# One level of Strassen's scheme for the gate features of a fused attention layer

## What is computed

```python
p = rmsnorm(x, g) @ w_in                 # (1088, 2048) x (2048, 10064)
qa, ka, va, qi, wi, ki, za, qb, kb, vb, zb, ga, gb = split(p)
score = sum_h relu(qi_h . ki) * wi_h      # the indexer
keep  = top_k(score, 256)                 # keys that each query of branch A attends to
oa = attend(qa, ka, va, keep, bias);  ob = window_attend(qb, kb, vb, sinks, bias)
m  = sigmoid(ga) * ((oa * silu(za)) @ w_br_a) + sigmoid(gb) * ((ob * silu(zb)) @ w_br_b)
y  = rmsnorm(x + m @ w_out, final_g)
```

## Time and profile before

| | |
|---|---|
| median of 3 runs | 3377.52 us (3373.89 to 3378.17) |
| the profiled execution: its own time | 3377.38 us |
| its span, first to last instruction | 3375.6 us |
| PE busy | 3148.7 us (93%) |
| DVE, ACT, POOL busy | 1325.3, 850.0, 881.5 us |
| mean granted TensorE clock | 0.967 |
| ACT cast of a 128x512 quarter, mean | 620 ns |
| DMA over the span | 91 GB/s |

### The profile page before, as it was taken

One profiled execution on the slowest core, in us unless ns is written; L12 is line 12 of the kernel. 1 busy time (PEld: TensorE's weight loads), 2 busy tenths in 40 slices (PEclk: granted clock), 3 DMA queues, 4 the chain that ended last, 5 costly groups with the idle time before them and its releaser, 6 DMA issues. The chain is left out here.

```text
span 3375.6 us, 47356 instructions
## 1 busy us (share of the span) xinstructions
PE 3148.7 (93%) x17837; PEld 2975.9 (88%) x17837; DVE 1325.3 (39%) x2169; ACT 850.0 (25%) x1753; POOL 881.5 (26%) x652
## 2 busy tenths in 40 slices
PE   5999999999999999999999987975778999999997
PEld 5999999999999999999999986754667999978875
DVE  5003362737282721695000007754994111120411
ACT  4112112131312212211011115533653111031422
POOL 1222211122121222122122214422552222143453
PEclk7999999999999999999999998986998999999999
DMA  4232322222222222222633224234325333263442
GB/s 145 81 98 61 84 62 70 79 64 79 59 69 76 61 79 74 58 63 77 103 98 87 80 64 118 57 88 91 69 55 161 117 111 115 72 227 101 143 159 100
DMA packets 356871, 308.47 MB, mean 91 GB/s; under 512 B 34744, under 2 KB 316440, under 8 KB 353224
## 3 DMA queue, kind: packets, MB, share of 16 engines
q1 hardware_dynamic: 328384, 244.02, 25.9%
q10 hardware_dynamic: 28360, 62.72, 6.6%
HBM read 232.31 MB, written 74.43 MB: 91 GB/s over the span
## 5 line engine op out<-in xcount | busy, mean ns | idle before, releaser
L594 PE MATMUL banks<-h_hi,w_in_tile_hi 128*128 128x384 f32 (+3 forms) x3664 | 823.4, 331 | 10.0 <-POOL w_in_tile_lo L464 7.5
L594 PE MATMUL banks<-h_lo,w_in_tile_hi 128*128 128x384 f32 (+3 forms) x3664 | 821.2, 330 | 0.0
L594 PE MATMUL banks<-h_hi,w_in_tile_lo 128*128 128x384 f32 (+3 forms) x3664 | 821.1, 330 | 0.0
L464 POOL TENSOR_TENSOR w_in_tile_lo<-w_in_tile_raw,w_in_tile_hi 128x512 fp32r<-128x512 f32 x312 | 406.2, 1303 | 1541.5 <-ACT w_in_tile_hi L484 1541.5
L594 PEld LDWEIGHTS banks<-h_hi,w_in_tile_hi 128*128 128x128 f32 (+1 forms) x3664 | 633.4, 188 | 23.0 <-POOL w_in_tile_lo L464 8.1
L594 PEld LDWEIGHTS banks<-h_hi,w_in_tile_lo 128*128 128x128 f32 (+1 forms) x3664 | 631.4, 187 | 1.2
L594 PEld LDWEIGHTS banks<-h_lo,w_in_tile_hi 128*128 128x128 f32 (+1 forms) x3664 | 628.5, 187 | 1.6
L484 ACT CAST w_in_tile_hi<-w_in_tile_raw 128x512 fp32r<-128x512 f32 x312 | 192.9, 620 | 1347.2 <-PE banks L594 1264.1
L761 DVE MAX8 top<-score 128x8 f32<-128x384 f32 (+6 forms) x224 | 247.1, 1103 | 33.0 <-DVE score L764 1.1
L764 DVE MATCH_REPLACE8 score<-top,score 128x384 f32<-128x384 f32 (+6 forms) x224 | 242.9, 1084 | 0.0
L2102 PE MATMUL banks<-w_out_tile_hi,m_hi 128*128 128x512 f32 x576 | 226.5, 393 | 14.9 <-DVE m_lo L2032 13.2
(11 more groups left out here) (243 smaller groups left out, 3570.3 us busy)
## 6 DMA issues: line engine op xcount, KB each, us to landing
w_in_tile_raw<-in_w_in SPq DMA_DIRECT2D x312, 256.0 KB, 2.9
product<-spill ACTq DMA_DIRECT2D x70, 544.0 KB, 3.4
w_out_tile_raw<-in_w_out SPq DMA_DIRECT2D x128, 256.0 KB, 3.1
u_b<-product SPq DMA_DIRECT2D x32, 544.0 KB, 6.2
merged<-u_b ACTq DMA_DIRECT2D x16, 544.0 KB, 7.4
x_rows<-in_x_prompt SPq DMA_DIRECT2D x8, 1024.0 KB, 5.3
b_q_raw<-product SPq DMA_DIRECT2D x16, 512.0 KB, 7.5
w_br_tile_raw<-in_w_br_b SPq DMA_DIRECT2D x64, 128.0 KB, 2.9
```

What stands on the lines that cost most here:

```text
L464: pool.tensor_tensor(s.w_lo[:, q, :, :], s.w_raw[:, q, :, :], s.w_hi[:, q, :, :].bitcast(F32), ALU.subtract).then_inc(lo_made, 1)
L594: last = pe.matmul(ps[0:m, 3 * slot + c, 0:w], w_[:, q, kq, 0:m], h_[:, k, t0:t0 + w], start=(k == 0 and w_ is s.w_hi and h_ is s.h_hi), s ...
```

## The change

The 32 gate tiles leave `project`, which is left with 46 tiles. `project` now also stores the normed rows (`h_hi + h_lo`, 16 times 128x1088) to a DRAM tensor `normed`. Three new stages read them back. They take the gate features in 16 pairs of tiles and the prompt as two halves of 512 tokens and two halves of 1024 features. `gate_sums` makes three products of sums (1024 features deep, 512 token columns each) per pair; `gate_half(t)`, for t = 0 and 1, makes two more per pair, each 576 columns (a token half and the 64 sample tokens) in two chunks of 288, and adds them to the parts that lie in `product`. Sigmoid moves from the evacuation to `merge` on ACT, silu becomes one ACT function in place of sigmoid on ACT and a multiplication on DVE, and the bias line and the turning of keys and values move into `gate_sums`.

```diff
+            (QA, 1, "copy", None), (QA + P, 1, "copy", 2), (QA + 2 * P, 2, "copy", None),
+            (QA + 4 * P, 1, "copy", 3), (QA + 5 * P, 3, "copy", None), (QA + 8 * P, 1, "copy", 4),
+            (QA + 9 * P, 3, "copy", None), (QB, 1, "copy", 5), (QB + P, 3, "copy", None),
+            (QB + 4 * P, 1, "copy", 6), (QB + 5 * P, 4, "copy", None), (QB + 9 * P, 1, "copy", 7),
+            (ZA, 4, "silu", None), ("sample keys", 0), (ZA + 4 * P, 1, "silu", None), ("sample keys", 1),
+            (ZA + 5 * P, 1, "silu", None), ("sample keys", 2), (ZA + 6 * P, 2, "silu", NB), (ZB, NB, "silu", None)]
...
+            def store_h_row(k):
+                sp.wait_ge(h_row_made, k + 1)
+                sp.dma_start(s.hT[k * P:(k + 1) * P, :], h_row).then_inc(h_row_stored, 16)
...
                     loop(sp, n0, count, lambda n, j, i: load_tile(n, j, i, col))
+                    if n0 == 1:
+                        for k in range(KT):
+                            store_h_row(k)
...
+            for k in range(KT):
+                if k:
+                    dve.wait_ge(h_row_stored, 16 * k)
+                dve.tensor_tensor(h_row, s.h_hi[:, k, :].bitcast(F32), s.h_lo[:, k, :].bitcast(F32),
+                                  ALU.add).then_inc(h_row_made, 1)
...
+def gate_sums(nc, s, w_in, rel_bias, one_hot, cache_b_k, cache_b_v, outs):
...
+        def _(pool):
+            def rows_lo(j):
+                for i in range(3):
+                    pool.wait_ge(a_hi_made, 3 * j + i + 1)
+                    pool.tensor_tensor(a_lo[:, i, j, :], mix[:, j % 2, i, :], a_hi[:, i, j, :].bitcast(F32),
+                                       ALU.subtract).then_inc(a_made, 1)
...
+            for j in range(HALF_K):
+                rows_lo(j)
+                if j < RING:
+                    split_lo(j)
+            for u in range(RING, UNITS):
+                split_lo(u)
...
+        def _(dve):
+            def mix_rows(j):
+                dve.wait_ge(rows_in[j % 2], 32 * (j // 2 + 1))
+                if j >= 2:
+                    dve.wait_ge(a_made, 3 * (j - 1))
...
+                    dve.tensor_tensor(mix[:, j % 2, i, :], x, y, op).then_inc(mixed, 1)
+            def sum_weights(u):
...
+                dve.tensor_tensor(w_sum[:, u % RING, :, :], x, y, ALU.add).then_inc(summed, 1)
...
+        def _(pe):
+            def product(n, i):
...
+                for half in range(2):
+                    u = 6 * n + 2 * i + half
+                    pe.wait_ge(lo_made, u + 1)
+                    for kq in range(KQ):
+                        k = KQ * half + kq
+                        if n == 0:
+                            pe.wait_ge(a_made, 3 * k + i + 1)
+                        for w_, a_ in ((w_hi, a_hi), (w_hi, a_lo), (w_lo, a_hi)):
+                            last = pe.matmul(ps[:, bank, :], w_[:, u % RING, kq, :], a_[:, i, k, :],
...
+def gate_half(nc, s, w_in, t):
...
+            def load_rows(j):
+                if j >= 2:
+                    sp.wait_ge(a_made, 2 * (j - 1))
...
+            def load_part(n):
+                if n >= 2:
+                    sp.wait_ge(part_stored[n % 2], 32 * (n // 2))
...
+                        if n == 0:
+                            pe.wait_ge(a_made, 2 * k + i + 1)
+                        for w_, a_ in ((w_hi, a_hi), (w_hi, a_lo), (w_lo, a_hi)):
+                            for c, (t0, w) in enumerate(CHUNKS):
+                                last = pe.matmul(ps[:, bank + c, 0:w], w_[:, u % RING, kq, :], a_[:, i, k, t0:t0 + w],
...
+            def sigmoids(slot, i):
+                act.wait_ge(g_in[slot], i * 32 + (16 * PAIRS // 2 + 32))
+                act.activation(gates[:, slot, :, :], gates[:, slot, :, :], ACT.Sigmoid).then_inc(sig_made, 1)
...
+        gate_sums(nc, s, ins["w_in"], ins["rel_bias"], ins["one_hot"], ins["cache_b_k"], ins["cache_b_v"], outs)
+        gate_half(nc, s, ins["w_in"], 0)
+        gate_half(nc, s, ins["w_in"], 1)
```

More of the change, by code:

```diff
@@ L71 @@
 ALL_SELECTED = TOPK
+HALF_T = SEQ // 2
+HALF_K = KT // 2
+GATE_PAIRS = D // P
 TCH_I = ((ALL_SELECTED, 416), (ALL_SELECTED + 416, 416))
@@ L456, in _ @@
                     load_queries(x)
-            sp.wait_ge(rolled, 32)
+            store_mask(NB)
         @block.gpsimd
@@ L496, in evacuate @@
                     else:
-                        last = act.activation(out, acc, ACT.Sigmoid)
-                last.then_inc(sigmoid_made if kind == "silu" else evacuated, 1)
+                        last = act.activation(out, acc, ACT.Silu)
+                last.then_inc(evacuated, 1)
                 act.wait_ge(evacuated, n + 1)
@@ L527, in tile @@
                             split_hi(n + 1, scored=None if scored is None else (scored, j, count))
-                        if kind == "silu" and j % 2:
-                            last = isinstance(n, int)
-                            store_block(NB - 1 if last else i + first_turned[col], load_next=not last)
                         slot = (n0 + j) % 2
@@ L619, in _ @@
                     loop(pe, n0, count, tile)
-                elif what == "bias line":
-                    pe.wait_ge(consts_in, 32)
-                    pe.matmul(ps[0:H_A + H_B, 7, 0:RELS], table, hot, start=True, stop=True).then_inc(line_done, 1)
-                elif what == "turn the sample":
-                    turn_block(0, DEC)
                 elif what == "natural":
@@ L768, in _ @@
                         mask_made, 1)
-                elif what == "bias line":
-                    dve.wait_ge(line_done, 1)
-                    dve.tensor_copy(line, ps[0:H_A + H_B, 7, 0:RELS]).then_inc(line_out, 1)
-                    dve.wait_ge(line_out, 1)
-                    dve.sem_inc(kv_copied, 1)
-                    dve.tensor_scalar(line_a, line[0:H_A, :], line[0:H_A, 0:1], None, ALU.subtract).then_inc(line_out, 1)
-                elif what == "turn the sample":
-                    dve.wait_ge(mask_out, 16 * len(blocks))
-                    copy_block(0, DEC)
-                elif what == "tiles" and x[3] == "silu":
-                    n0, col, count, _, _ = x
-                    seen = sum(g[1] for g in groups if g[2] == "silu" and g[0] < col)
-                    def gate(n, j, i):
-                        if j % 2:
-                            b0 = first_turned[col]
-                            dve.wait_ge(kv_stored, i * (16 * BLOCK_STORES) + 16 * (SAMPLE_STORES + BLOCK_STORES * b0))
-                            copy_block(i + (b0 + 1), P)
-                        slot = (n0 + j) % 2
-                        dve.wait_ge(sigmoid_made, i * 2 + (seen + j + 1))
-                        for c, (t0, w) in enumerate(TCH):
-                            last = dve.tensor_tensor(spill[:, slot, t0:t0 + w], ps[:, 3 * slot + c, 0:w],
-                                                     spill[:, slot, t0:t0 + w], ALU.mult)
-                        last.then_inc(evacuated, 1)
-                    loop(dve, n0, count, gate)
```

512 lines of the change are left out of this document (427 added, 85 removed).

## The result

The changed kernel takes 3556.34 us (median of 4 runs, 3554.06 to 3559.81), the kernel before beside it 3376.85: ratio 1.0534, 95% interval 1.0515 to 1.0552. It is slower, by 180 us where 170 were forecast. The profiled run took 3554.06 us, its span is 3552.3 us, 176.7 longer than before.

The account below looks back on a forecast made before the run. The prediction took PE as the bound, above all in `project`. Its terms -94 + 47 + 57 + 21 + 119 + 20 = +170 us on 3377.4 gave 3547 us, range 3450 to 3630.

Parts of the forecast that it names:

- Matmuls, -94 us: Gate products: 32 tiles of 24.0 us become 16 pairs of 16.4 + 25.7 us, 768 to 674 us.
- no gain by smaller matmuls: Rival for the gate products: 288 columns still take 0.167 us, +101 us, 3650 us; chance 0.04.
- no fixed part: Rival for the new stages: a matmul's fixed part is nearly nothing, 59 us less, about 3490 us; chance 0.03.
- Steady pairs paced by DMA: Rival for the new stages: at 135 GB/s a gate_half pair takes 17.6 us, +150, 3700 us; chance 0.08.
- Rows to DRAM, +47 us: In project after tile 2: 16 one-buffer stores at 4.9 us a turn delay tile 3's weights; stall 45 us, clock 2.
- The milder case: Rival: waits in project partly hidden, or fills in the new stages without sharing; 3495 to 3440 us, chance 0.18.
- Masks and queries, +57 us: In project: fewer tiles between scored blocks, so PE waits 16, 1, 10, 18, 3 and 3 us, plus clock.
- Boundaries and fills, 21 + 119 = +140 us: New stages: three boundaries of 7 us each; operand fills of 53 us in gate_sums and 33 us twice in gate_half.
- The sharing of DVE and POOL: Fill of gate_sums: each DVE operation lengthens POOL's work by 0.6 us, k-tiles taking 7.6, later 5.7 us.
- Bias lines, +20 us: In gate_sums: two line stores hold ACT's queue; PE waits some 3 us, then 27, 2 for clock, against 8 before.
- Sigmoid in `merge`, 0: In merge: two more ACT tiles, some 2 us against 24 us of PE work, cost nothing; 32 us if uncovered.
- rival of PE as the bound throughout: Rival for the whole kernel: only work and boundaries change, -94 + 21, 3304 us; chance 0.03.

Follow-up runs that it names:

- b1_rows: The kernel before with only the 16 additions of h_hi and h_lo and their stores to DRAM put in, read by nothing: 3412.09 us, ratio 1.0109.
- e1_rows3: The changed kernel with the 16 rows of h stored to DRAM through three buffers instead of one: 3524.47 us, ratio 1.0428.
- b2_dense: The kernel before with only the new spacing of the scored blocks, all 18 gate tiles behind, gates made as before: 3437.68 us, ratio 1.0179.
- e2_lines8: The changed kernel with the replicated store of the bias lines cut into 8 parts, one in each of 8 pairs: 3518.14 us, ratio 1.0416.
- c3_all: c1_all with the first six weight units' low parts in gate_sums also on DVE and each new stage's first weights in two loads: 3431.38 us, ratio 1.0172.
- e4_dve_lo: The changed kernel with the low parts of the summed operand tiles in gate_sums subtracted on DVE instead of POOL: 3554.15 us, ratio 1.0517.
- e7_fill: The changed kernel with e4_dve_lo, first pairs' products side by side by k-tile, weight units earlier, three row buffers in gate_half: 3542.01 us, ratio 1.0498.
- c1_all: The changed kernel with e1_rows3, e2_lines8, e7_fill and one late silu tile moved between scored blocks 5 and 6: 3449.23 us, ratio 1.0209.

## Why the prediction was right

The forecast of 3547 us is 9 us under the measured 3556, by terms that can now be set beside what ran.

- **Matmuls, -94 us.** 288 columns follow each other at 0.133 us (two matmuls in 0.26 and 0.27 us, timeline of PE):

```profile
1850.15 0.42 PE L1211 MATMUL banks<-gh_a_lo,gh_w_hi 128*128 128x288 f32 x2
1850.41 0.43 PE L1211 MATMUL banks<-gh_a_hi,gh_w_lo 128*128 128x288 f32 x2
1850.68 0.42 PE L1211 MATMUL banks<-gh_a_hi,gh_w_hi 128*128 128x288 f32 x2
```

  In the trace of the changed kernel eleven pairs of `gate_half` in a row start 12.80 us apart (1752.3 to 1893.1), and the pairs of `gate_sums` without transposes 16.32, where 12.9 and 16.4 were reckoned; with transposes it is 17.01. So the term is 16 x (16.32 + 25.60) - 768 = -97. The rivals of no gain by smaller matmuls (0.167 us each) and of no fixed part (0.12) are out. One of the prediction's bounds is a slip: at 0.167 us the term would be +7, as its own rival has it (-94 + 101), and not -10. The gap of N / 2.4 + 2.5 ns that the Trainium skill gives in TensorE: Matmul & The Clock Gate, section Back-to-back issue gap, is not what this kernel shows: by it 512 columns would take 0.216 us (an estimate), and the traces have 0.227 to 0.23. That section calls it the gap of an isolated matmul; for a stream with weight loads between, which this kernel is, it has some 131 ns at 512 columns, and no run here comes near that.
- **Steady pairs paced by DMA, the rival of 3700 us.** It is out: from 1765 to 1940 PE is busy for 174.05 of 175 us beside 180 GB/s.
- **Rows to DRAM, +47 us: measured +37 (b1_rows, e1_rows3).** Mechanism, place and order right, the turn mis-sized: 3.98 us and not 4.9. The 3.4 us were taken from stores of the earlier trace rows that ran beside loads; with nothing else on the queues a store of the same size landed after 2.6. The milder case, that later waits hide part of it, is out by b1_rows, where `project` ends 37 us later; its other half, fills without sharing, is out by the lockstep.
- **Masks and queries, +57 us: measured +60 (b2_dense).** In the changed kernel the waits were 17.3, 2.5, 10.2, 19.0, 3.3 and 3.3 us for 16, 1, 10, 18, 3 and 3.
- **Boundaries and fills, 21 + 119 = +140 us: +141.** The stages of 327.2 us (e2_lines8, without the lines' cost), 246.0 and 245.3 us less 16 steady pairs each (and 7 us of transposes in the first, which `project` had before) leave 59, 41 and 41. Up to the end of the first pair it is 54, 40 and 40 us in the changed kernel, where 60, 40 and 40 were forecast; the other 7 are slower pairs further on, for which the prediction had nothing. The sharing of DVE and POOL, +0.6 us for each operation, was right in kind; the pairs of operations took 1.68 us as in lockstep, which gives 6.7 and 5.05 us a k-tile where 7.6 and 5.7 were reckoned.
- **Bias lines, +20 us: 39 us of waits and 40 by e2_lines8, some +32 against the 8 of before.** The step that was short is the one from the second hold to PE's next weights: the prediction let PE have them at 47 to 54 us. The hold ended 51 us after the first store, but behind it stood five small stores of 2.3 to 4.0 us each, 17.3 us in all, and PE had its weights at 71. It also had no wait of 7.2 us for `gs_kv`, whose loads on SP landed after some 20 us beside the same packets, and after some 2 in e2_lines8.
- **Sigmoid in `merge`, 0.** What follows the gates takes 1361.2 us, before 1361.5. PE's work in `merge` stretches over 395.6 us instead of 393.5, so at most 2 us of it show and not the 32 of sigmoids uncovered: as good as hidden, as forecast.

The sum of the measured terms is -97 + 37 + 60 + 141 + 32 = +173, within 4 us of the traces' 176.7. The 10 us that the rows had too much and the 12 that the lines had too little balanced each other, and so did the 6 of the first fill and the 7 of the slower pairs; that the total is so close is luck to that extent.

The rival of PE as the bound throughout, 3304 us, was to be decided at 73 us of waits. With the causes eased, in c3_all, the losses are still 58 + 97 = 155 us, twice that: PE's waits over 1.5 us in the trace of c3_all are 51 us at the boundaries, 35 for masks and queries and 25 within the stages, 111 in all. What the other 44 us are (the lower clock behind the waits, shorter waits, slower pairs) was not measured.

## What to carry to other kernels

A scheme that saves matmuls has to be charged for every operand that must be made before PE's first product of a new stage, and for the work that its tiles were hiding: here 97 us of matmuls were bought with 97 us of hiding and staging in `project` and 173 us in and between the new stages. When several engines feed PE, the wait list names the last one; the cause is found by following its idle time upstream to a buffer, a queue or a shared path. A single staging buffer in a chain of add and store costs its landing time each turn, and a store that repeats a line many times is best issued in parts: here the engine behind its queue paid, and not the transfer (e2_lines8).

## What the runs showed of the hardware

- DVE and POOL, both with two inputs from SBUF: where DVE waits for POOL's results they go in turn, 1.68 us a pair (0.63 and 1.27 alone). Where DVE has work without a gap, POOL does not get on: one subtraction of 512 columns took 22.08 us in e4_dve_lo, 13.03 in e7_fill and 10.03 in c1_all (the first of two that took 11.26). Each of the three ended 1.12 to 1.14 us after DVE's first gap, which is nearly all of the 1.26 us that POOL needs alone. The prediction had POOL's operations 0.7 us longer for each of DVE's; there DVE was not busy throughout.
- Two stores of 1.5 and 3 MB, a line repeated 128 times, held ACT's queue 10.13 us at the issue of the second, 26.24 us at the next store and 2.3 to 4.0 us at each of the six behind it; cut in eight, an issue took 0.36 to 0.66 us.
- Stores of 544 KB landed after 2.6 us where nothing else was on the queues, after 3.4 in the median beside loads.
